# Operands of TensorE's products at other byte offsets in SBUF: activations in cells, low parts of the weights 12 or 32 bytes in

## The reference, cut to what matters

```
h = rms_norm(x, ffn_norm_g[l])
u = causal_dwconv(h @ ffn_w_in[l], ffn_conv_w[l]) + ffn_conv_b[l]
gate, up = split(u)
x = x + (silu(gate) * up) @ ffn_w_out[l]
```

```
x = x + 0.5 * rms_norm(swiglu(rms_norm(x), ff1_w_in[i], ff1_w_out[i]))
x = x + rms_norm(mixer(rms_norm(x)))
x = x + 0.5 * rms_norm(swiglu(rms_norm(x), ff2_w_in[i], ff2_w_out[i]))
swiglu(h, w_in, w_out) = (silu(gate) * up) @ w_out,   gate, up = split(h @ w_in)
```

## Time and profile before

| | |
|---|---|
| Time before | 2537.78 us, median of 3 runs (2536.23 to 2538.86) |
| The profiled execution | 2536.61 us, of which the span of the trace is 2534.8 us |
| TensorE products | 2518.7 us busy (99% of the span), 15209 of them |
| Weight loads (PEld) | 2223.5 us (88%) |
| VectorE | 1769.4 us (70%) |
| ScalarE | 1395.5 us (55%) |
| GpSimd | 150.6 us (6%) |
| Granted TensorE clock | 1.00 over the whole span |
| Weights moved | 459.47 MB, mean 181 GB/s |

### The profile page before, as it was taken

The page is one execution under the profiler, slowest core; times in us unless marked ns, Lnnn a source line. Parts: engine busy times, 40 slices in busy tenths (PEclk is TensorE's granted clock), DMA queues, the critical chain, the costliest instruction groups (busy, mean ns, idle before and its releaser), DMA issues.

```text
span 2534.8 us, 37208 instructions
## 1 busy us (share of the span) xinstructions
PE 2518.7 (99%) x15209; PEld 2223.5 (88%) x15209; DVE 1769.4 (70%) x2500; ACT 1395.5 (55%) x2078; POOL 150.6 (6%) x228
## 2 busy tenths in 40 slices
PE   9999999999999999999999999999999999999999
PEld 9999888998888988888888888888988888898887
DVE  7778567885775777757657775775777577567773
ACT  7766476664554555545555554554555455455553
POOL 2100011000000000000010000002010000010000
PEclk9999999999999999999999999999999999999999
DMA  7266552664665556556564655655456556563763
GB/s 224 98 178 211 173 166 84 189 194 166 208 196 197 181 162 194 189 187 197 185 221 147 204 192 187 195 187 196 153 166 201 188 180 205 184 207 125 216 189 127
DMA packets 543027, 459.47 MB, mean 181 GB/s; under 512 B 10634, under 2 KB 500058, under 8 KB 542858
## 3 DMA queue, kind: packets, MB, share of 16 engines
q1 hardware_dynamic: 537351, 441.52, 54.9%
q0 software_dynamic: 4656, 15.30, 1.7%
q10 hardware_dynamic: 851, 0.28, 0.0%
HBM read 455.97 MB, written 1.10 MB: 180 GB/s over the span
## 4 chain that ended last, share of the span: by engine, by line
PE 95%; DVE 3%; ACT 1%; DMA 1%; issue 0%; POOL 0%; DVEq 0%; POOLq 0%; ACTq 0%
PE ps L964 28%; PE ps L847 23%; PE ps L846 11%; PE ps L829 5%; PE ps L830 5%; PE ps L831 5%; PE ps L784 2%; PE ps L783 2%; PE ps L782 2%; PE ps L765 2%; PE ps L766 2%; PE ps L767 2%; PE ps L849 1%; PE ps L687 1%; DVE wlo L1956 1%; PE ps L1065 1%
## 5 line engine op out<-in xcount | busy, mean ns | idle before, releaser
L1956 DVE TENSOR_TENSOR wlo<-raw,whi 128x2048 fp32r<-128x2048 f32 (+1 forms) x419 | 956.7, 2287 | 363.2 <-ACT whi L1362 363.1
L1362 ACT ACTIVATE whi<-raw 128x2048 fp32r<-128x2048 f32 (+2 forms) x421 | 800.3, 1906 | 293.2 <-DMA raw<-in_ff_w_out 161.1
L847 PE MATMUL ps<-h,whi 128*128 128x512 f32 x2560 | 873.6, 393 | 0.0
L846 PE MATMUL ps<-h,wlo 128*128 128x256 f32 x2240 | 629.7, 281 | 0.0
L847 PEld LDWEIGHTS ps<-h,whi 128*128 128x128 f32 x2560 | 459.7, 188 | 81.5
L846 PEld LDWEIGHTS ps<-h,wlo 128*128 128x128 f32 x2240 | 421.9, 188 | 15.3
L1362 ACT ACTIVATE u<-ps 128x512 f32<-128x512 f32 x160 | 96.0, 600 | 397.4 <-PE ps L847 397.4
L964 PE MATMUL ps<-whi,hid_hi 128*128 128x512 f32 x880 | 291.3, 390 | 0.0
L964 PE MATMUL ps<-whi,hid_lo 128*128 128x512 f32 x880 | 290.7, 389 | 0.0
L964 PE MATMUL ps<-wlo,hid_hi 128*128 128x512 f32 x880 | 290.3, 389 | 0.0
L829 PE MATMUL ps<-h,whi 128*128 128x256 f32 x1024 | 288.1, 281 | 0.0
(11 more groups left out here) (337 smaller groups left out, 3285.9 us busy)
## 6 DMA issues: line engine op xcount, KB each, us to landing
raw<-in_ff_w_in SPq DMA_DIRECT2D x160, 1024.0 KB, 5.6
raw<-in_ff_w_out SPq DMA_DIRECT2D x88, 1024.0 KB, 4.8
raw<-in_ffn_w_in SPq DMA_DIRECT2D x40, 1024.0 KB, 5.6
raw<-in_a_w_qkv SPq DMA_DIRECT2D x24, 1024.0 KB, 5.0
raw<-in_ffn_w_out SPq DMA_DIRECT2D x22, 1024.0 KB, 4.8
raw<-in_w_in SPq DMA_DIRECT2D x18, 1024.0 KB, 6.2
raw<-in_ff_w_in SPq DMA_DIRECT2D x32, 512.0 KB, 4.4
raw<-in_c_w_qkv SPq DMA_DIRECT2D x12, 1024.0 KB, 5.0
```

Source lines behind the costliest of these rows:

```text
L846: e.matmul(out[:, 0:SEQ], lo, m.h[:, 0, k, :], start=False, stop=False, skip_group_check=True)
L847: ins = e.matmul(view(out, a=2), hi, m.h[:, :, k, :], start=(k == 0), stop=(k == KT - 1), skip_group_check=True)
L1362: return self.nc.scalar.activation(*a, **k)
L1956: self.e.tensor_tensor(chunk_view(m.wlo[:, slot, :], c), chunk_view(m.raw[:, slot, :], c), chunk_view(m.whi[:, slot, :], c).bitcast(F32), ...
```

## The change

It changes where operands lie, and no product's shape.

1. `h` gets the shape (2, 8, 2, 128 + 16): a cell for each part, block and token tile, of 144 floats (576 bytes, a multiple of 64), with 128 used. The used floats begin at 0 for the gated stages and for the operand of an output product (`H_AT["swiglu"]`, `H_AT["out"]`), and 8 floats (32 bytes) in for `mix1`, `mix2` and `ffn1`. The moving operand of L847 is then four runs of 128 floats in place of two of 256; that of L846 and L829 to L831 two runs in place of one.
2. A slot of `raw` and `wlo` gets 16 floats more (2064). The data of a chunk begin 3 floats (12 bytes) in for chunks of the gated stages that multiply `h`, 8 floats (32 bytes) in for those of `mix1`, `mix2` and `ffn1`, and at 0 for the last chunks of every stage, which go into `block`. The DMA writes there, and the split reads and writes there. `whi` stays at 0.
3. The two fillers around `h` go. The values of one mixer (`v_mla`) get places inside other memory, to make room.
4. In the second `mix1` ScalarE takes the first bank out of PSUM as soon as the first factor of the norm is there, then rounds the chunk, then waits for the second factor and takes out the second bank.

```diff
+H_AT = {"out": 0, "mix1": 8, "mix2": 8, "ffn1": 8, "swiglu": 0}
+PAD = 16
+LOW_IN = 8
+LOW_SWIGLU = 3
...
+    def take(self, stage):
+        self.inputs = self.m.h_at(stage)
...
-                hi, lo = w_of(m.whi[:, c % SLOTS, :], f, k), w_of(m.wlo[:, c % SLOTS, :], f, k)
+                hi, lo = w_of(m.whi[:, c % SLOTS, :], f, k), w_of(low(m.wlo, c), f, k)
                 if k > 0:
-                    e.matmul(out[:, 0:SEQ], lo, m.h[:, 0, k, :], start=False, stop=False, skip_group_check=True)
-                ins = e.matmul(view(out, a=2), hi, m.h[:, :, k, :], start=(k == 0), stop=(k == KT - 1), skip_group_check=True)
+                    e.matmul(view(out[:, 0:SEQ], a=TT), lo, self.inputs[:, 0, k, :, :], start=False, stop=False, skip_group_check=True)
+                ins = e.matmul(out.rearrange("p (a t c) -> p a t c", a=2, t=TT), hi, self.inputs[:, :, k, :, :], start=(k == 0), stop=(k == KT - 1), skip_group_check=True)
...
-        if l > 0:
-            self.split(0, 0)
-        e.wait_ge(s.rstd, TT * self.rounds["norm"])
         if l == 0:
+            e.wait_ge(s.rstd, TT * self.rounds["norm"])
             keep(0)
             self.split(0, 0)
             keep(1)
         else:
             for t in range(TT):
+                e.wait_ge(s.rstd, TT * (self.rounds["norm"] - 1) + t + 1)
                 self.evict_head(t, proj, C_CQ, HEAD_WIDTH, ACT.Copy)
+                if t == 0:
+                    self.split(0, 0)
...
+def low_places():
+
+    out = []
+    for stage in PLAN:
+        n, rows = chunks_of(stage), 4 if stage[0] in ("mix1", "mix2") else FT // 2
+        out += [LOW_SWIGLU if stage[0] == "swiglu" else LOW_IN] * (n - rows) + [0] * rows
+    return out
+
+
+def low(a, c):
+
+    return a[:, c % SLOTS, LOW_AT[c]:LOW_AT[c] + CW]
...
-            [("raw", [P, SLOTS, CW])],
-            [("wlo", [P, SLOTS, CW], F32R)])
-        sb(ctx, "in_front_of_h", [P, 8])
-        m.h = sb(ctx, "h", [P, 2, KT, SEQ], F32R)
-        sb(ctx, "behind_h", [P, 120])
-        m.h_hi, m.h_lo = m.h[:, 0, :, :], m.h[:, 1, :, :]
+            [("raw", [P, SLOTS, CW + PAD])],
+            [("wlo", [P, SLOTS, CW + PAD], F32R)])
+        m.h = sb(ctx, "h", [P, 2, KT, TT, P + PAD], F32R)
+        m.h_at = lambda stage: m.h[:, :, :, :, H_AT[stage]:H_AT[stage] + P]
+        m.out_hi, m.out_lo = (m.h_at("out")[:, i, :, :, :] for i in range(2))
```

More of the change, by code:

```diff
@@ L756, in tokens_tile @@
         c = self.c0 + b
-        whi, wlo = (a[:, c % SLOTS, :].rearrange("p (k c) -> p k c", k=KT)[:, :, 0:w] for a in (m.whi, m.wlo))
+        whi, wlo = (a.rearrange("p (k c) -> p k c", k=KT)[:, :, 0:w] for a in (m.whi[:, c % SLOTS, :], low(m.wlo, c)))
         out = m.ps[:, self.bank(b), t * 256:t * 256 + w]
@@ L772, in pair_tile @@
         c = self.c0 + b
-        whi, wlo = (a[:, c % SLOTS, 0:PAIR * w].rearrange("p (k c) -> p k c", k=PAIR) for a in (m.whi, m.wlo))
+        whi, wlo = (a[:, 0:PAIR * w].rearrange("p (k c) -> p k c", k=PAIR) for a in (m.whi[:, c % SLOTS, :], low(m.wlo, c)))
         out = m.ps[:, t, 0:w]
@@ L823, in features_chunk @@
                 between()
-            out = m.ps[:, self.bank(b), f * 256:(f + 1) * 256]
+            out = view(m.ps[:, self.bank(b), f * 256:(f + 1) * 256], a=TT)
             for k in range(KT):
@@ L999, in down @@
         self.by_group, self.what = False, kind
-        self.blocks(range(FT // 2), (self.m.hid_hi, self.m.hid_lo, 4), True)
+        hi, lo = (a.rearrange("p f (t c) -> p f t c", t=TT) for a in (self.m.hid_hi, self.m.hid_lo))
+        self.blocks(range(FT // 2), (hi, lo, 4), True)
     def out(self, what, l):
@@ L1004, in out @@
             self.begin_out(what)
-        self.blocks(OUT_ORDER[what], (self.m.h_hi, self.m.h_lo, 0), False)
+        self.blocks(OUT_ORDER[what], (self.m.out_hi, self.m.out_lo, 0), False)
     def begin_out(self, what):
@@ L1128, in mix @@
         if r == 1:
+            self.take("mix1")
             self.begin_product()
@@ L1395, in split_first @@
         self.e.wait_ge((s.first_landed, s.landed[0])[half], 16)
-        whi, raw = (chunk_view(a[:, 0, :], 0)[:, 4 * half:4 * half + 4, :] for a in (m.whi, m.raw))
+        whi, raw = (chunk_view(a, 0)[:, 4 * half:4 * half + 4, :] for a in (m.whi[:, 0, :], low(m.raw, 0)))
         self.act(whi, raw, ACT.Copy).then_inc((s.first_hi, s.split_hi)[half], 1)
@@ L1419, in square_new, with turn_hi @@
         self.square_half(t, half, self.m.x[:, t, half * 512:(half + 1) * 512])
-    def turn_hi(self, t, gain, only=None):
+    def turn_hi(self, t, gain, stage, only=None):
         m, s = self.m, self.s
+        h_hi = m.h_at(stage)[:, 0, :, :, :]
         if t == 1 and only is None:
@@ L1484, in edge @@
             self.square_sum(1, 0)
-            self.turn_hi(0, gain)
+            self.turn_hi(0, gain, after[0])
             self.square_x(0)
             self.square_sum(1, 1)
-            self.turn_hi(1, gain)
+            self.turn_hi(1, gain, after[0])
             self.split(2, 0)
@@ L2009, in rotary_angles, with turn_lo @@
         e.tensor_scalar(m.ang[:, :], m.ang0[:, :], lim, -lim, ALU.min, ALU.max).then_inc(s.angles, 1)
-    def turn_lo(self, t, gain, only=None):
+    def turn_lo(self, t, gain, stage, only=None):
         e, m, s = self.e, self.m, self.s
+        h_hi, h_lo = (m.h_at(stage)[:, i, :, :, :] for i in range(2))
         if t == 1 and only is None:
@@ L2051, in split_first @@
         self.e.wait_ge((s.first_hi, s.split_hi)[half], 1)
-        whi, wlo, raw = (chunk_view(a[:, 0, :], 0)[:, 4 * half:4 * half + 4, :] for a in (m.whi, m.wlo, m.raw))
+        whi, wlo, raw = (chunk_view(a, 0)[:, 4 * half:4 * half + 4, :] for a in (m.whi[:, 0, :], low(m.wlo, 0), low(m.raw, 0)))
         self.e.tensor_tensor(wlo, raw, whi.bitcast(F32), ALU.subtract).then_inc((s.first_lo, s.split_lo)[half], 1)
@@ L2112, in edge @@
             if after is not None:
-                self.turn_lo(0, gain)
+                self.turn_lo(0, gain, after[0])
             self.weigh_sum(1, 1, weight)
@@ L2116, in edge @@
             if after is not None:
-                self.turn_lo(1, gain)
+                self.turn_lo(1, gain, after[0])
         else:
```

104 lines of the change are left out of this document (55 added, 49 removed).

## The result

The changed kernel takes 2557.27 us (median of 4 runs, 2556.03 to 2559.42) against 2537.31 us for the kernel before: ratio 1.0079, 95% interval 1.0062 to 1.0097, so 20 us slower. The forecast was 2510 us, and the range ended at 2545.

What follows compares the result with a forecast made beforehand. TensorE's own product rate was taken to bound the kernel. Gains of 15.4 + 3.7 + 1.7 + 3.7 + 2.3 + 1.0 = 27.8 us against the median of 2537.78 gave 2510 us, range 2488 to 2545.

Steps and rivals of the forecast that it cites:

- What bounds the kernel now: Opening step: TensorE's product rate sets the stages, operand places set that rate, with floors 226.8 ns (512 columns) and 113.4 (256).
- `features_chunk`: `ffn1` and attention, 3072 products at 116.7 ns: 1.2 ns less each, -3.7 us, bounds 10 us either way.
- `pair_tile`: In front of gated stages, 384 of 720 products: 232.3 to 228 ns, -1.7 us, bounds -2.1 and +1.0.
- Rows 6: Trace of gated pairs at 353 then 347 ns within one round of k, read as a sign that operand places count.
- the rival in which the change does nothing: Gated pairs stay at 349 ns and only the order in `mix1` gains: 2537 us, chance 0.08.
- `wide_chunk`: Gated stages, 2560 pairs: 349 to 343 ns, -15.4 us, bounds -23 (340 ns) and +15 (355 ns).
- The doubt about the 12 bytes: Rival that the new places are worse: gated pairs at 355 ns, 2540 us, or 2554 with `features_chunk` at its ceiling; chance 0.10.
- `tokens_tile`: 1536 products at 118.3 ns: 1.5 ns less each, -2.3 us, bounds -7.5 and +3 us.
- `block` after a mixer: 528 products with `h` moved to 0: 7.1 ns less each, -3.7 us, bounds that and 0.
- Second `mix1`: First bank taken out before the chunk's rounding: TensorE starts 1.4 us earlier; term -1.0 us, bounds -1.4 and +0.5.
- DMA: Rival in gated stages: chunks landing 12 bytes off a line make DMA the bound, about 2800 us at twice the time; chance 0.05.
- The port rule: Skill's rule that weight loads steal no read bandwidth from a running matmul; by it offsets change nothing, time close to before.

Runs made afterwards that it cites:

- e7: The kernel before with `hid` 256 bytes past a multiple of 512, by a shorter filler behind `h` (56 floats); 2538.42 us in one execution.
- e8: The kernel before with `hid` 128 bytes past a multiple of 512, by a shorter filler behind `h` (24 floats); 2550.73 us in one execution.
- e1: The changed kernel with a 192-byte filler behind `h`, putting `hid` back at a multiple of 512 bytes; 2550.13 us.
- e5: Of the change only the 8256-byte slot pitch and the order in the second `mix1`; `h`, `hid` and low parts placed as before; 2546.66 us.
- e2: The kernel before with only `hid` moved to 320 bytes past a multiple of 512, by a shorter filler; 2555.23 us.
- e3: The kernel before with `h` also at a multiple of 512 bytes, like `whi`, `wlo` and `hid`; 2542.51 us.
- e4: The changed kernel with low parts and raw weights at 0 in place of 12 and 32 bytes in; 2550.86 us.
- e12: The kernel before with `raw` and `wlo` 12 bytes in for all chunks, slots still 8192 bytes apart; 2553.49 us in one execution.
- e6: Of the change only the cells of `h`, used part 32 bytes in for all stages, and the order in the second `mix1`; 2540.31 us.
- e10: The kernel before with `h` 64 bytes past a multiple of 512 in place of 32; 2540.78 us in one execution.
- e11: The kernel before with `h` 128 bytes past a multiple of 512 in place of 32; 2546.43 us in one execution.

## Why the prediction was wrong

**The step that failed** is the one under "What bounds the kernel now", where the earlier trace rows give "`hid` lies at 0 and `h` 32 bytes in" as the whole difference and 0 means a multiple of 64 bytes. Both large errors follow from it: that a buffer moved by a multiple of 64 costs nothing, and that 226.8 ns, with half of it for 256 columns, is the floor of every shape "at 0". Between the forecast (27.8 us less) and the trace (21.0 us more) lie 48.8 us. 19.8 of them are the gated pair (-15.4 forecast, +4.4 measured), 13.7 the outward product of the feed-forwards, which has no term in the sum, 7.6 `features_chunk`, 3.9 `block` and `pair_tile`, and the rest small terms and the start of the kernel.

**`block` after a feed-forward.** `hid` was at a multiple of 512, `whi` and `wlo` were too; e7 and e8 show that the rate repeats with 256 bytes. With the right unit the change is seen to move more than it names: `hid` to 320 past a multiple, the slots and the cells by 64 a step. The unpriced 13.7 us come from `hid` and the slots together: put back singly, `hid` gives 7.4 (after against e1), and what is left, 6.3, is what the slots cost alone (e5). Moved alone, `hid` costs 17.3 (e2), so these shares hold only in this order.

**Rows 6.** The prediction took the pairs of 353 and 347 ns in the earlier trace rows as a sign that places count, and against the rival in which the change does nothing. In the unit of 256 bytes no operand moves there from one k to the next: the blocks of the weights are 512 bytes apart, those of `h` 1024. In the mean of 304 rounds the first four pairs of the kernel before take 352.1 ns and the last four 346.7, so the difference is real, but the place within 256 bytes cannot be its cause, and no run here looked for the cause. That places do count is shown by e2; that the earlier trace rows pointed there was luck.

**`wide_chunk`.** I took -15.4 us; it was +4.4. The floor of 340 ns a pair was not reached at these places: e3 has both products at the places of the earlier trace rows and takes 901.9 us, 349.8 ns a pair. The number that was most off is the 226.8 ns for 512 columns, which take 234.0 in this pair. The half, which I had called an estimate, was off less here: 256 columns take 115.8 ns in the pair against 113.4. In `ffn1` they take 120.0. Of the change's parts the 12 bytes cost 5.3 us (e4, e12), the slots 2.7 alone (e5), the cells 0.5 alone (e6); without the 12 bytes the rest together gains 0.9 us. The doubt about the 12 bytes was in a rival. That its 2554 us come near the measured 2557.27 is luck: they were made of a pair at 355 ns and `features_chunk` at its ceiling, where the pair is at 351.0 in the mean and the largest loss was in neither.

**`features_chunk`.** I took -3.7 us with bounds of 10 either way; it was +2.8 and +1.1, from cells and slots. The credit for moving `wlo` to the same 32 bytes was empty (e4: 228.8 against 228.6).

**`tokens_tile`.** I took -2.3 us; nothing came of it. Its 256-column products start 119.7 ns apart before and after (mean of 1410 intervals).

**`block` after a mixer, and `pair_tile`.** -3.7 and -1.7 forecast, -1.5 measured together (-2.9 with 1.4 for the order in `mix1`). The direction was right and the size wrong, for the same reason: cells 576 bytes apart are at the place of the earlier trace rows only in one of four. With whole blocks at 0 it is -6.2 (e3), though there the `pair_tile` products that I had left at 32 bytes moved as well.

**Second `mix1`.** 1.4 us earlier, and 0.4 us left waiting for the low part at L772, both as worked out. Nothing was given back: the stretch behind it, up to the outward product, took 92.06 us in place of 92.02.

**DMA.** The rival was wrong in its effect and not in its direction: share 0.71 against 0.65 in the gated stage, landing 6.2 against 5.6 us, still no wait. Two parts of the change lengthen the landing, each alone: the slot pitch (e5 6.1 us) and the 12 bytes (e12 6.2 us). The cells do not (e6 5.6 us).

**The port rule.** e2 differs from the kernel before in the length of a filler, and its outward products, which wait for nothing, take 17.3 us longer. In e5 and in the changed kernel the rate goes by where the loaded and the streamed operand lie against each other. The Trainium skill ("TensorE: Matmul & The Clock Gate", Part 2, Step-by-step) has load and stream on two independent ports with no stealing; by that alone their places against each other would not matter, and here they do. Nor do the 16-byte lines of "SBUF — State Buffer", Door 1, explain it: 0, 32, 64, 128 and 320 bytes are all whole lines and cost 226.8 to 233.9 ns in `block` (233.9 at 32, 232.4 at 128, 233.5 at 320). What inside the memory makes the difference was not measured, and I leave it open.

## What to carry to other kernels

When TensorE never waits, compare start to start of the same shape between stages. A difference is a reason to suspect the place of operands and no proof of it (the earlier trace rows had one without any). Move one buffer by a filler and nothing else, as e2 does; if the rate changes, every buffer's address is part of the kernel, fillers included. List the address of each operand before and after a change, modulo more than the unit that you believe in, also for buffers that the change does not name. A rate that one shape reaches at some places is no floor for another shape: try it alone first.

## What the runs showed of the hardware

- 512-column `float32r` products with a load under each take 226.8 ns in `block` when stationary and moving operand both begin at a multiple of 256 bytes (before, e3, e7). With the stationary operand elsewhere they take 233.9 ns at 32 bytes, 232.4 at 128 (e8) and 233.5 at 320 (e2).
- The places count against each other: with `hid` at 0 a chunk whose `wlo` is at 0 takes 226.8 ns a product and one at 64 takes 230.0 (e5); with `hid` 64 past a multiple of 256 it is 233.3 and 231.1 (changed kernel).
- A rate is that of a shape in its sequence: the 512-column products of the gated pair take 234.0 ns at the places where `block` has 226.8 (e3).
- 256-column products behave otherwise: in `ffn1` 120.0 ns at equal places and 116.7 with the moving operand 32 bytes on; in the gated pair 115.8 and 118.0. All are above half of 226.8.
- A low part 12 bytes in costs in either role: 1.1 us of 60.8 in an outward product, 0.7 us of 112.6 in a gated one (e12).
- Chunks of 1 MB land in 5.6 us with slots 8192 bytes apart, in 6.1 us with slots 8256 bytes apart (e5), and in 6.2 us with slots 8192 bytes apart and the data 12 bytes in (e12).
- The effects of two moves do not add: cells +4.2, slots +1.6, both +2.8 us in `ffn1`; `hid` +17.3, slots +6.3, both +13.7 us in the outward products.
- After a wait of 1.8 us on TensorE the granted clock fell to 0.50 for 3.4 us in four traces (e2, e7, e10, e11) and stayed full in four others (before, e3, e8, e12); in e2 and e7, where the second `mix1` had no other change, it cost 1.5 us.
